# Expert weights in two-k-tile chunks of 1024 columns, with two column blocks run together

## The reference, cut to what matters

```python
for e in range(N_EXPERTS):                       # 8
    g, u = split(xf @ w_gate_up[e])              # (256,1024) @ (1024, 2*3584)
    y += combine[:, e:e+1] * ((silu(g) * u) @ w_down[e])   # (3584,1024)
```

## Time and profile before

| | us |
|---|---|
| time, median of 3 runs | 2134.93 |
| the three runs | 2134.93, 2135.71, 2125.97 |
| span of the profiled execution, first to last instruction | 2123.7 |
| its own time beside the span | not given apart; the runs are 2.3 to 12.0 above the span |

### The profile page before, as it was taken

How to read it: one execution, slowest core, us unless ns; L and a number is a source line. 1 busy time by engine, 2 the same in 40 slices (tenths; PEclk the granted TensorE clock), 3 DMA queues, 4 the chain that set the end, 5 groups by cost and what they waited for, 6 DMA issues and landing times.

```text
span 2123.7 us, 25981 instructions
## 1 busy us (share of the span) xinstructions
PE 1955.9 (92%) x9673; PEld 1625.0 (77%) x9673; DVE 1397.3 (66%) x1154; ACT 1145.9 (54%) x1009; POOL 58.8 (3%) x81
## 2 busy tenths in 40 slices
PE   7967999898889998877899999999999999999997
PEld 6756997685569986676687888878788787788875
DVE  3444775432254455454787888878888787888874
ACT  4333554343434333332576776767677776677762
POOL 1230000200000000000000000000000000000000
PEclk9958999896679999957799999999999999999997
DMA  6603455440034554401598999999999999899980
GB/s 227 197 30 138 158 193 185 141 165 21 0 134 169 197 178 159 139 1 60 204 363 310 351 350 334 351 321 358 341 334 348 331 354 332 316 352 337 362 296 35
DMA packets 251586, 486.86 MB, mean 229 GB/s; under 512 B 14108, under 2 KB 19292, under 8 KB 251536
## 3 DMA queue, kind: packets, MB, share of 16 engines
q1 hardware_dynamic: 244976, 477.30, 63.8%
q0 software_dynamic: 6560, 8.91, 1.4%
HBM read 484.05 MB, written 1.05 MB: 228 GB/s over the span
## 4 chain that ended last, share of the span: by engine, by line
PE 60%; DVE 13%; DMA 12%; ACT 8%; issue 4%; DVEq 2%; ACTq 0%; SPq 0%; POOL 0%; POOLq 0%
DMA w_raw<-in_moe_w_down 8%; PE psum L1759 8%; PE psum L1761 7%; PE psum L1760 7%; DVE w_lo L834 7%; PE psum L1416 7%; PE psum L1417 7%; PE psum L1418 6%; ACT w_hi L512 5%; DMA w_raw<-in_moe_w_gate_up 4%; PE psum L1447 3%; PE psum L1434 2%; PE psum L1437 2%; PE psum L1436 2%; PE psum L1802 1%
## 5 line engine op out<-in xcount | busy, mean ns | idle before, releaser
L834 DVE TENSOR_TENSOR w_lo<-w_raw,w_hi 128x2048 fp32r<-128x2048 f32 (+2 forms) x475 | 1031.7, 2200 | 384.1 <-ACT w_hi L512 381.1
L512 ACT ACTIVATE w_hi<-w_raw 128x2048 fp32r<-128x2048 f32 (+2 forms) x475 | 863.8, 1842 | 269.4 <-DMA w_raw<-in_moe_w_gate_up 103.8
L1759 PE MATMUL psum<-w_hi,xg_hi 128*128 128x512 f32 x896 | 360.3, 402 | 1.3 <-DVE w_lo L834 0.8
L1761 PE MATMUL psum<-w_hi,xg_lo 128*128 128x512 f32 x896 | 354.9, 396 | 0.0
L1760 PE MATMUL psum<-w_lo,xg_hi 128*128 128x512 f32 x896 | 354.8, 396 | 0.0
L1434 PE MATMUL psum<-xt_hi,w_hi 128*128 128x256 f32 x704 | 198.6, 282 | 3.8 <-DVE w_lo L834 2.1
L1761 PEld LDWEIGHTS psum<-w_hi,xg_lo 128*128 128x128 f32 x896 | 168.7, 188 | 41.0
L1759 PEld LDWEIGHTS psum<-w_hi,xg_hi 128*128 128x128 f32 x896 | 169.0, 189 | 40.2 <-DVE w_lo L834 1.7
L1760 PEld LDWEIGHTS psum<-w_lo,xg_hi 128*128 128x128 f32 x896 | 169.1, 189 | 38.0
L1436 PE MATMUL psum<-xt_lo,w_hi 128*128 128x256 f32 x704 | 197.9, 281 | 0.0
L1437 PE MATMUL psum<-xt_hi,w_lo 128*128 128x256 f32 x704 | 197.7, 281 | 0.0
(11 more groups left out here) (336 smaller groups left out, 2104.6 us busy)
## 6 DMA issues: line engine op xcount, KB each, us to landing
w_raw<-in_moe_w_gate_up SPq DMA_DIRECT2D x224, 1024.0 KB, 6.7
w_raw<-in_moe_w_down SPq DMA_DIRECT2D x96, 1024.0 KB, 6.7
w_raw<-in_w_up SPq DMA_DIRECT2D x22, 1024.0 KB, 5.7
w_raw<-in_ffn_w_gate_up SPq DMA_DIRECT2D x22, 1024.0 KB, 5.5
w_raw<-in_moe_w_down SPq DMA_DIRECT2D x32, 512.0 KB, 4.3
w_raw<-in_w_in SPq DMA_DIRECT2D x12, 1024.0 KB, 6.3
w_raw<-in_ab_w_in SPq DMA_DIRECT2D x12, 1024.0 KB, 5.4
w_raw<-in_w_down SPq DMA_DIRECT2D x10, 1024.0 KB, 6.5
```

Source lines behind the costliest of these rows:

```text
L512: return act.activation(o, i, func, **kw)
L834: TT(w_lo[:, k % RING, 0:n], w_raw[:, k % RING, 0:n], w_hi[:, k % RING, 0:n].bitcast(F32), ALU.subtract)\
L1759: mm(o, hi[:, q, :], wh, start=(q == first), stop=False)
L1761: m = mm(o, lo[:, q, :], wh, start=False, stop=(q == last))
```

## The change

Gate and up run in rounds of two column blocks: three rounds with chunks of 2 k tiles by 1024 columns (rows of 4096 bytes), four chunks for gate into banks 0 and 1, four for up into banks 2 and 3, and a last round with the seventh block as before. Down runs both halves of the output together: chunks of 2 k tiles by 1024 columns, twelve full and, at the very end, four of one k tile (half-size). There are still 44 chunks. ACT's silu and DVE's product take two blocks at once in the first three rounds; ACT no longer waits for the gate before it rounds on. PE turns two blocks over after the first chunk of the next round. Both `ys` halves are made after the last chunk.

```diff
--- before.py
+++ after.py
@@ -99,10 +99,12 @@
     ]
 
 
-MOE_PAIRS = D_EXP // NB
-MOE_DOWN = [4] * 6 + [2, 2]
-MOE_UP_CHUNKS = MOE_PAIRS * 4
-MOE_CHUNKS = MOE_UP_CHUNKS + 2 * len(MOE_DOWN)
+MOE_BLOCKS = D_EXP // NB
+MOE_PAIRS = MOE_BLOCKS // 2
+MOE_ROUNDS = MOE_PAIRS + 1
+MOE_DOWN = [2] * 12 + [1] * 4
+MOE_UP_CHUNKS = MOE_BLOCKS * 4
+MOE_CHUNKS = MOE_UP_CHUNKS + len(MOE_DOWN)
 
 
 def build(nc, a, out, upto="end"):
@@ -235,13 +237,13 @@
             ("ppt_lo", [P, 2, SEQ], F32R))
         (sig, p_out) = layout(at_phase, ("sig", [P, 2, NT, NB], F32), ("p_out", [P, NT, D], F32))
 
-        (xn_hi, xn_lo, xg_hi, xg_lo, mh_hi, mh_lo, mg, mh, rw) = layout(
+        (xn_hi, xn_lo, xg_hi, xg_lo, mh_hi, mh_lo, mh, rw) = layout(
             at_phase, ("xn_hi", [P, NT, D], F32R), ("xn_lo", [P, NT, D], F32R), ("xg_hi", [P, KD, P], F32R),
             ("xg_lo", [P, KD, P], F32R), ("mh_hi", [P, KE, P], F32R), ("mh_lo", [P, KE, P], F32R),
-            ("mg", [P, NB], F32), ("mh", [P, 2, NB], F32), ("rw", [P, KD, N_EXP], F32))
-        (ys_hi, ys_lo, sel, selt, gslot) = layout(
+            ("mh", [P, 2, NB], F32), ("rw", [P, KD, N_EXP], F32))
+        (ys_hi, ys_lo, sel, selt, mg, gslot) = layout(
             at_xt, ("ys_hi", [P, D], F32R), ("ys_lo", [P, D], F32R), ("sel", [P, NT, P], F32R),
-            ("selt", [P, SEQ], F32R), ("gslot", [P, 1], F32))
+            ("selt", [P, SEQ], F32R), ("mg", [P, 2, NB], F32), ("gslot", [P, 1], F32))
 
         psum = ctx.enter_context(nc.psum_tensor("psum", [P, 8, NB], F32))
         acc = [[psum[:, 2 * s + t, :] for t in range(NT)] for s in range(2)]
@@ -268,7 +270,7 @@
         def item_width(k):
 
             down = MOE_UP_CHUNKS <= k < MOE_CHUNKS
-            return NB * MOE_DOWN[(k - MOE_UP_CHUNKS) % len(MOE_DOWN)] if down else CHUNK
+            return 2 * NB * MOE_DOWN[k - MOE_UP_CHUNKS] if down else CHUNK
 
         block = ctx.enter_context(nc.Block())
 
@@ -342,18 +344,18 @@
                 def expert(e, r):
 
                     k = N_BEFORE_MOE
-                    for j in range(MOE_PAIRS):
-                        for n0 in (j * NB, D_EXP + j * NB):
-                            for k0 in (0, 4):
-                                load(k, r, moe_up[bass.ds(e, 1), k0 * P:(k0 + 4) * P, n0:n0 + NB]
-                                     .rearrange("e (k p) n -> p (e k) n", p=P), 4, NB)
+                    for q in range(MOE_ROUNDS):
+                        nk, n = (2, 2 * NB) if q < MOE_PAIRS else (4, NB)
+                        for n0 in (2 * q * NB, D_EXP + 2 * q * NB):
+                            for k0 in range(0, KD, nk):
+                                load(k, r, moe_up[bass.ds(e, 1), k0 * P:(k0 + nk) * P, n0:n0 + n]
+                                     .rearrange("e (k p) n -> p (e k) n", p=P), nk, n)
                                 k += 1
-                    for n0 in (0, NB):
-                        k0 = 0
-                        for nk in MOE_DOWN:
-                            load(k, r, moe_down[bass.ds(e, 1), k0 * P:(k0 + nk) * P, n0:n0 + NB]
-                                 .rearrange("e (k p) n -> p (e k) n", p=P), nk, NB)
-                            k, k0 = k + 1, k0 + nk
+                    k0 = 0
+                    for nk in MOE_DOWN:
+                        load(k, r, moe_down[bass.ds(e, 1), k0 * P:(k0 + nk) * P, :]
+                             .rearrange("e (k p) n -> p (e k) n", p=P), nk, 2 * NB)
+                        k, k0 = k + 1, k0 + nk
 
                 with sp.Fori(0, N_EXP) as i:
                     expert(i, i * R_ITEM)
@@ -774,29 +776,35 @@
                 copy(selt[:], scr[:, 2, 0:SEQ])
                 copy(gslot[:], scr[:, 2, SEQ:SEQ + 1]).then_inc(S("selt_ready"), 1)
 
+            def turned_hi(i, j):
+                act.wait_ge(S("mh_t"), MOE_BLOCKS * i + j + 1)
+                copy(mh_hi[:, 4 * j:4 * j + 4, :], psum[:, 6 + j % 2, :].rearrange("p (k n) -> p k n", n=P))\
+                    .then_inc(S("mh_hi_ready"), 1)
+
             def item(i):
                 c0, r = N_BEFORE_MOE, i * R_ITEM
-                for j in range(MOE_PAIRS):
-                    wait_used(act, c0 + 4 * j + 2, r)
-                    if j:
-                        act.wait_ge(S("mh_ready"), MOE_PAIRS * i + j)
-                    copy(mg[:], psum[:, 2 * (j % 2), :], ACT.Silu).then_inc(S("mg_ready"), 1)
-                    rounds(4 * j + 4, 4 * j + 6, r)
-                    if j:
-                        act.wait_ge(S("mh_t"), MOE_PAIRS * i + j)
-                        copy(mh_hi[:, 4 * j - 4:4 * j, :], psum[:, 6 + (j - 1) % 2, :].rearrange("p (k n) -> p k n", n=P))\
-                            .then_inc(S("mh_hi_ready"), 1)
-                    rounds(4 * j + 6, 4 * j + 8, r)
-                j = MOE_PAIRS
-                act.wait_ge(S("mh_t"), MOE_PAIRS * i + j)
-                copy(mh_hi[:, 4 * j - 4:4 * j, :], psum[:, 6 + (j - 1) % 2, :].rearrange("p (k n) -> p k n", n=P))\
-                    .then_inc(S("mh_hi_ready"), 1)
-                k = 4 * j + 4
+                for q in range(MOE_PAIRS):
+                    rounds(8 * q + 4, 8 * q + 6, r)
+                    if q:
+                        turned_hi(i, 2 * q - 2)
+                        turned_hi(i, 2 * q - 1)
+                    rounds(8 * q + 6, 8 * q + 8, r)
+                    wait_used(act, c0 + 8 * q + 4, r)
+                    copy(mg[:], psum[:, 0:2, :], ACT.Silu).then_inc(S("mg_ready"), 1)
+                    rounds(8 * q + 8, 8 * q + 12, r)
+                k = 8 * MOE_PAIRS + 4
+                rounds(k, k + 2, r)
+                turned_hi(i, MOE_BLOCKS - 3)
+                turned_hi(i, MOE_BLOCKS - 2)
+                wait_used(act, c0 + 8 * MOE_PAIRS + 2, r)
+                copy(mg[:, 0, :], psum[:, 0, :], ACT.Silu).then_inc(S("mg_ready"), 1)
+                rounds(k + 2, k + 6, r)
+                turned_hi(i, MOE_BLOCKS - 1)
+                k, end = k + 6, MOE_CHUNKS
+                rounds(k, end + 2, r)
+                k = end + 2
+                wait_used(act, c0 + end, r)
                 for n in range(2):
-                    end = MOE_UP_CHUNKS + len(MOE_DOWN) * (n + 1)
-                    rounds(k, end + 2, r)
-                    k = end + 2
-                    wait_used(act, c0 + end, r)
                     copy(ys_hi[:, n * NB:(n + 1) * NB], psum[:, 4 + n, :], scale=gslot[:, 0:1])\
                         .then_inc(S("ys_hi_ready"), 1)
                 take_item(i + 1, k, r)
@@ -1243,27 +1251,36 @@
                 dve.wait_ge(S("gathered"), 3 * n + 2)
                 dve.tensor_copy(xg_lo[:], psum[:, 2:4, :].rearrange("p b (k n) -> p (b k) n", n=P)).then_inc(S("xg_ready"), 1)
 
+            def gated_h(i, q, n):
+                dve.wait_ge(S("mg_ready"), MOE_ROUNDS * i + q + 1)
+                wait_used(dve, N_BEFORE_MOE + 8 * q + 4 * n, i * R_ITEM)
+                dve.wait_ge(S("mh_t"), MOE_BLOCKS * i + 2 * q)
+                TT(mh[:, 0:n, :], mg[:, 0:n, :], psum[:, 2:2 + n, :], ALU.mult).then_inc(S("mh_ready"), 1)
+
             def item(i):
-                c0, r = N_BEFORE_MOE, i * R_ITEM
-                for j in range(MOE_PAIRS):
-                    splits(4 * j + 4, 4 * j + 6, r)
-                    if j:
-                        lo_h(i, j - 1)
-                    dve.wait_ge(S("mg_ready"), MOE_PAIRS * i + j + 1)
-                    wait_used(dve, c0 + 4 * j + 4, r)
-                    if j >= 2:
-                        dve.wait_ge(S("mh_t"), MOE_PAIRS * i + j - 1)
-                    TT(mh[:, j % 2, :], mg[:], psum[:, 2 * (j % 2) + 1, :], ALU.mult).then_inc(S("mh_ready"), 1)
-                    splits(4 * j + 6, 4 * j + 8, r)
-                    if j == 1:
+                r = i * R_ITEM
+                for q in range(MOE_PAIRS):
+                    splits(8 * q + 4, 8 * q + 6, r)
+                    if q:
+                        lo_h(i, 2 * q - 2)
+                        lo_h(i, 2 * q - 1)
+                    splits(8 * q + 6, 8 * q + 10, r)
+                    gated_h(i, q, 2)
+                    splits(8 * q + 10, 8 * q + 12, r)
+                    if q == 0:
                         dve.wait_ge(S("gathered"), 3 * i + 3)
                         select(i + 1)
-                lo_h(i, MOE_PAIRS - 1)
-                k = 4 * MOE_PAIRS + 4
+                k = 8 * MOE_PAIRS + 4
+                splits(k, k + 2, r)
+                lo_h(i, MOE_BLOCKS - 3)
+                lo_h(i, MOE_BLOCKS - 2)
+                gated_h(i, MOE_PAIRS, 1)
+                splits(k + 2, k + 6, r)
+                lo_h(i, MOE_BLOCKS - 1)
+                k, end = k + 6, MOE_CHUNKS
+                splits(k, end + 2, r)
+                k = end + 2
                 for n in range(2):
-                    end = MOE_UP_CHUNKS + len(MOE_DOWN) * (n + 1)
-                    splits(k, end + 2, r)
-                    k = end + 2
                     dve.wait_ge(S("ys_hi_ready"), 2 * i + n + 1)
```

(64 more changed lines are left out.)

## The result

The changed kernel is slower: 2141.44 us median of 9 runs (2133.25 to 2146.37), against 2130.97 (2125.51 to 2135.71) for the kernel before on the same chip. The ratio is 1.0054, with a 95% interval of 1.0034 to 1.0074. I had forecast 2120.6 and a range of 2107 to 2138: the time is outside it, and of the wrong sign. A second set of runs on another chip gave 1.0045 [1.0022, 1.0068]. The profiled execution of after has a span of 2140.3, that of before 2123.7. Those 16.6 us are more than the medians differ by, because the profiled execution of before is one of its quicker ones; what follows explains spans.

The account below looks back on a forecast made before the run. PE was taken to bound gate and up, with down losing time to a drained ring. Terms -10.2 (down), -1.1 (chunk 4), -4.9 and +1.9 (ends) summed to -14.3 us: 2120.6 against a median of 2134.93, range 2107 to 2138.

Parts of the forecast that it names:

- The item's end: From an item's last down matmul to the next item: -4.9 us over seven ends, +1.9 at the eighth.
- With a lead of 2.8: At the item's end, w_lo is done 2.8 us before PE wants the chunk, giving next item at E + 6.9.
- 44 lands after about 5.6: The next item's first load, 44, lands about 5.6 us after issue: 5.2 plus some queueing behind 43.
- 45 one transfer (2.8) behind it: The next item's second load lands 2.8 us after load 44; w_hi and w_lo then add 4.35.
- Two ys_lo in a row put the scatter 0.75 later: At the item's end, making both ys halves after the last chunk delays the scatter 0.75 us behind the same w_lo.
- The clock: After shorter waits at item ends PE's lower clock loses 1.5 us; half of one such loss counted as saved.
- Rival 2: Slower: four half chunks starve the item's end, 10.2 us for 7.5; +10, about 2145; chance 0.15.
- Down drain: In the middle of down, the ring's drain behind two half chunks goes: -10.2 us.
- Chunk 4: First item's gate and up: ACT no longer stops before silu, so PE's wait for chunk 4 goes; -1.1 us.
- Gate and up 81.0, transposes at nothing, wide products: Gate and up stay 81.0 us per item; transposes' new wait costs 0; wide products at most 1.4 us each.
- Longer rows, 4%: Chunk loads with 4096-byte rows take 4% less, 2.8 us per chunk; saves nothing itself but holds the lead near 3.
- rival 3: Chunk loads: memory, not packets, sets the rate, so the time is about 2129; chance 0.05.

Follow-up runs that it names:

- halves_front: The changed kernel with down's four half chunks at the start of down, not at its end; 2130.53 us, 1.0005 of the kernel before.
- halves_spread: The changed kernel with down's four half chunks spread, one in each group of four chunks; 2126.19 us, 0.9985 of the kernel before.
- up_only_order: Changed gate and up, old down part, chunk 45's splits behind the last ys part (DVE's behind the first y add); 2129.98 us, 0.9997 of before.

## Why the prediction was wrong

**The step that failed is "The item's end", -4.9 + 1.9.** It came out at +25.8: +25.7 in the first seven ends, where -4.9 was forecast, and +0.1 in the last. By its own terms, for a mean end of the first seven:

- "With a lead of 2.8". The lead at chunk 39 was 2.0. By the prediction's formula (E - 8.4 - lead + 1.2) load 44 leaves at E-9.2, and it left at E-9.1: the formula was right, and the lead 0.8 too large. I took the lead from the transfers' rate alone.
- "44 lands after about 5.6 (the 5.2 just named and some queueing behind 43)". It took 7.1. This is 1.5 us of the miss, and its source is in how I used: 5.21 was the time of load 45, behind the full load 44 that had left 2.7 us ahead of it. The load to look at was 44, the one behind half chunks; it took 5.5 us in the mean before, with 43 leaving 2.8 us ahead of it, and 43 now leaves 1.1 us ahead.
- "45 one transfer (2.8) behind it", then 4.35 for w_hi and w_lo: measured 2.7 and 4.35. Right. So w_lo of 45 ends at E+5.1 for E+2.75.
- "Two ys_lo in a row put the scatter 0.75 later". Right: the shortest distance from w_lo of 45 to the next item is 3.57 us in before (five ends) and 4.24 in the kernels with the new down part, 0.67 more.
- The clock. I counted 1.5 us for a loss and "half of one such loss as saved". Instead it was paid in all ends: over those shortest distances the mean end had 2.05 us in after and 0.43 in before. The added matmuls took all of the 2.05 away and cost 0.5 of their own. The earlier trace rows had the mark, PEclk 0.71 in the last end; I priced its return as unlikely, because I believed that waits would shorten.

Together for a mean end, against before: 1.38 for w_lo, 0.67 for the second ys_lo, 1.62 for the clock, 3.67, which is what the gap grew by. In the last end the forecast +1.9 is there, from E to the first matmul of the next layer: 11.95 us before (2060.62 to 2072.57), 13.83 after (2076.01 to 2089.84). But before, that layer's first nine matmuls still ran at the lower clock, and after they did not, which gives 1.5 back and leaves 14.1 for 14.0.

**Rival 2 is what happened**, a starved end, with its place and mechanism right and its size of the same kind: an end of 10.2 against 11.4, a time of 2145 against 2141, and its sign, a wait for ys_lo of over 2 us an item, at 3.4. I gave it 0.15, for a reason that the runs refute: "PE then does 7 us of other work, as cover". The cover is only the 3.5 us of gathers, since the scatter needs ys. And its point of decision, a lead under 1.2, was wrong: at 2.0 the end starved already.

**Down drain, -10.2.** Right: -10.3, with down at 39.63 us in each item. But the gain was a loan. The halves' drain did not go, it moved to the end; halves_front and halves_spread show that it is paid wherever the halves stand.

**Chunk 4, -1.1.** Wrong in its cause. The stop of ACT before mg is gone, and PE stands for chunk 4 as long as in the earlier trace rows, the one wait of this kind in the first item. PE and DVE after:

```profile
1040.50 0.50 PE L1778 MATMUL psum<-w_hi,xg_hi 128*128 128x512 f32 x1 [0.88 <-DVE w_lo L842]
...
1038.16 8.90 DVE L842 TENSOR_TENSOR w_lo<-w_raw,w_hi 128x2048 fp32r<-128x2048 f32 x4 [1.40 <-issue]
```

w_hi of chunk 4 now ended at 1033.2, 5.0 us before DVE took it up: DVE was at the routing until 1036.8 and began w_lo at 1038.16. It was the same before (routing until 1038.2, w_lo from 1039.56). The end of ACT's wait of 88.1 us did not shorten gate and up. What it came with is lead: w_lo of chunk 4 was done 3.8 us ahead of PE in items two to eight, where it was 0.85.

**Gate and up 81.0, transposes at nothing, wide products.** Right for this kernel: 81.0, 1.0 us in two waits, a product of 1.22 us. up_only_order shows that the transposes' wait is real once items start with leads of 0.5 to 1.4, as the formula's condition of 1.4 had it.

**Longer rows, 4%.** The queue in 1500 to 1520 us, beside the earlier trace rows:

```profile
q1 hardware_dynamic: 1842, 7.12, 96.5%
```

A full chunk takes 0.965 x 20 / 7.12 x 1.0486 = 2.84 us; the same way gives 2.92. That is 2.7% less, not 4. Other stretches of 20 us spread: 2.84 and 2.87 after, where nearly all rows are long (from 2020 and from 1860 us), and 2.89 to 2.97 before (from 1340, 1500, 1600 and 1860 us). The 2.85 us worked out from the Trainium skill ("DMA: Bandwidth & Descriptors", Why small descriptors are slow) agrees with it. By the prediction the lead would settle near 2 at that rate, and it was 2.0 at chunk 39; that the rate alone sets it was not tested. In rival 3, no limit by memory showed: the second of the two stretches above moved 1.61 MB in 4 us, 402 GB/s.

## What to carry to other kernels

In a ring with a fixed number of slots, half-size transfers halve what is under way; in this kernel they cost a refill wherever they stood, so place them last only if what follows does not need the next loads early. Count as cover only the work that does not itself depend on what is late. A wait of 4 us on TensorE costs more than 4 us, since what follows runs at the lower clock: look at PEclk in the stretch, and price its loss in every repetition. Matmuls added to fill such a wait pay as far as the wait is there anyway, and cost where it is shorter than they are. And a gain in lead can be spent once: an order that uses it up takes it from the loop that needed it.

## What the runs showed of the hardware

- Twelve matmuls without use, 2.8 us of work in an idle stretch, made the kernel 10 and 11 us faster, on two chips. With a wait of 4.43 us in front the scatter ran at 0.45 us a step; after filler work and 1.15 us of waiting it ran at 0.25, first step included. In the seven ends of after, with waits of 2.0 to 4.7 us, the gap was 2.05 us over the shortest distance in the mean.
- A full load behind two or more half ones landed 4.4 to 5.5 us after the last of them in the mean, behind a single one 3.7 to 4.1, and 2.7 at the same place where a full one stood ahead of it. Whether it was issued 1.1 or 2.8 us after the load ahead made no difference (4.5 and 4.4). In the stretch looked at, the packets in between took 0.20 us instead of 0.16.
- Leaving the next load for 1.9 us later did not quicken the one ahead of it.
